# The recurrent mixer's three gate-branch subtractions, from VectorE to GpSimd

## The chip, the core and the metric

The kernel runs on one core of a Trainium2 chip. What counts is the device time of one execution in microseconds (us), taken as the median of several runs; lower is better. The core has TensorE (PE in the profile), VectorE (DVE), ScalarE (ACT) and GpSimd (POOL), and SyncE (SP), whose queue issues the transfers from memory.

## What is computed

Two blocks of two layers each work on 256 tokens of width 1024 in float32. The part that the change touches is the recurrent mixer of the first block, cut here to its core:

```python
def mixer_rglru(h, w_in, conv_w, conv_b, w_a, b_a, w_x, b_x, lam, w_out):
    gate, xr = jnp.split(h @ w_in, [D_RNN], axis=-1)
    gate = jax.nn.gelu(gate)
    xr = causal_conv(xr, conv_w) + conv_b
    r = sigmoid(einsum('bthi,hij->bthj', xh, w_a) + b_a)     # xh: xr by heads
    i = sigmoid(einsum('bthi,hij->bthj', xh, w_x) + b_x)
    log_a = (LRU_C * r) * log_sigmoid(lam)
    a = exp(log_a)
    b = sqrt(-expm1(2.0 * log_a)) * (i * xr)
    hseq = scan(a, b)                                        # h_t = a_t h_(t-1) + b_t
    return (gate * hseq) @ w_out
```

Before it stand another mixer and a mixture of 32 experts, behind it a second mixture of experts (`moe1`), and then the second block (feed-forward, attention and pooling).

## The kernel before

Five programs run side by side, one for each engine and one for the transfer queue, each a list of instructions in a fixed order. They meet at counting semaphores: an instruction raises one when it ends, and another engine's program waits for a count. Nothing plans the order at run time. What stands behind a waiting instruction on its own engine waits too.

**Chunks.** A dense weight comes in chunks of 128 x 2048 float32 (1 MB), into a ring of six places (`dense_ring`). Chunk n goes to place n modulo 6 once its predecessor there has been used. The mixer's chunks are named `("lru", n)`: 0 to 3 are the input columns of the convolution branch, then come `c_w_a` and `c_w_x`, 4 to 7 are the input columns of the gate branch, 8 to 11 the output matrix.

**High and low halves.** To multiply in near float32 accuracy, each chunk is split. ScalarE rounds it to `w_hi` (the helper `hi`, L923), then VectorE computes the chunk less its `w_hi` as `w_lo` (the helper `lo`, L1283): a `tensor_tensor` subtraction with both inputs and the output in SBUF. Each goes in two halves f = 0, 1 of 128 x 1024. There are two buffers for such pairs, used in turn, so `hi` of a chunk waits until TensorE has multiplied the same half of the chunk two turns earlier. TensorE makes three products for each piece (L445 to L447), and `tile_products` waits for `("remainder", key, f)` before each half; its 24 products for one half need both `w_hi` and `w_lo`.

**The mixer's order.** TensorE: chunks 0 to 3, chunk 4, the 32 gate products with `c_w_a` and `c_w_x` (L598), chunks 5, 6, 7, then the output chunks 8 to 11. VectorE (`lru` in `dve_program`): the norm; `lo` of 1; constants (`decay`); four times `lo` of chunk 2 + j and then the convolution of two channels, each one `tensor_scalar` (L1439) and three `scalar_tensor_tensor` (L1442) that read two SBUF tensors; then `lo` of 6; `factors` (L1449, L1451, L1452) for pairs 0 and 1; `lo` of 7; `factors` for pairs 2 and 3; `lo` of 8; the scans (L1460, L1462); the gating (L1467, L1289); `lo` of 9. ScalarE follows a like order: `hi` of chunk 2 + j and a copy of the products; `hi` of 6; a gelu (L1043); 16 tanh (L1065) once the last convolution channel, `("xr", 7)`, is there; `factors` 0 and 1 (tanh L1049, exponential L1054); `hi` of 7; `factors` 2 and 3; `hi` of 8; the square roots (L1074).

**GpSimd** has only sums of squares and, far later, the pooling. Ahead of the mixer its queue holds `first_sums("moe0")`, behind it `first_sums("moe1")`, two additions of 128 x 512 (L1878, L1880).

**The transfer queue** (`sp_program`) waits for `remainder` of a place's old chunk before it loads the next one: the load of 10 waits for 4, that of 11 for 5. The first three expert matrices of `moe1` in the dense ring (`EXTRA`) wait for 6 and 7, for 8 and 9, for 10 and 11. The rest of the experts' matrices start when TensorE has finished chunk 11 (L1982).

Of the kernel before, what the change touches and what calls it, by code (L numbers as in the profile page):

```python
# [161 lines left out]
def build(nc, a, out, known):  # L162
# [5 lines left out]
    def signal(name, step=1):  # L168
        s = Signal(nc, name, known, step)
        signals.append(s)  # L170
        return s
# [2 lines left out]
    rounded = signal("rounded")  # L174
    acted = signal("acted")
    remainder = signal("remainder")
    vec = signal("vec")
    pooled = signal("pooled")
    x_loaded, consts_loaded, small_loaded = (signal(n, 16) for n in ("x_loaded", "consts_loaded", "small_loaded"))
# [139 lines left out]
    halved = [key for key, _, split in chunks if split]  # L319
    turn = {key: n for n, key in enumerate(halved)}  # L320
    splits = set(halved)

    def slot(key):
        return dense_ring[place_of[key]]
# [110 lines left out]
    def pe_program(_):  # L435
# [38 lines left out]
        def tile_products(key, b, ready, x=h_halves, ks=range(KD)):  # L474
            w = weights(key)
            for f in range(2):
                PE.wait_ge(remainder, key, f)
                for n, k in enumerate(ks):
                    PE.wait_ge(*ready(k))
                    ins = triple(bank[b][:, f * T:(f + 1) * T], [v[:, f, k, :] for v in w],  # L480
                                 [v[:, k, :] for v in x], n == 0, n == KD - 1)
                ins.then_inc(products.up(key, f), 1)
# [796 lines left out]
    def dve_program(_):  # L1279
        def lo(key, halves=(0, 1)):  # L1280
            for f in halves:
                DVE.wait_ge(rounded, key, f)
                V.tensor_tensor(half_of(key, f, 1), tile_of(slot(key), key, f), half_of(key, f, 0).bitcast(F32),  # L1283
                                ALU.subtract).then_inc(remainder.up(key, f), 1)
# [145 lines left out]
        def lru():  # L1430
            norm("lru")
            lo(("lru", 1))
            seq(V.memset(lru_pad[:, :, 0:PAD_C], 0.0), "pad")
            decay()
            for j in range(4):
                lo(("lru", 2 + j))
                DVE.wait_ge(acted, "xr", j)
                for c in (2 * j, 2 * j + 1):
                    seq(V.tensor_scalar(lru_xr[:, c, :], lru_pad[:, c, 0:T], small_of("c_conv_w", c, 1),  # L1439
                                        small_of("c_conv_b", c, 1), ALU.mult, ALU.add))  # L1440
                    for tap in (1, 2, 3):
                        seq(V.scalar_tensor_tensor(lru_xr[:, c, :], lru_pad[:, c, tap:tap + T],  # L1442
                                                   small_of("c_conv_w", tap * KD + c, 1), lru_xr[:, c, :], ALU.mult, ALU.add),
                            *(("xr", c) if tap == 3 else ()))
            lo(("lru", 6))

            def factors(g):
                DVE.wait_ge(acted, "tanh", g, 1)
                seq(V.scalar_tensor_tensor(pair(lru_bx, g), pair(lru_bx, g), 1.0, pair(lru_xr, g), ALU.add, ALU.mult))  # L1449
                DVE.wait_ge(acted, "ra", g)  # L1450
                seq(V.tensor_tensor(pair(lru_xr, g), pair(lru_ra, g), pair(lru_ra, g), ALU.mult))  # L1451
                seq(V.scalar_tensor_tensor(pair(hT, g), pair(lru_xr, g), 1.0, pair(hT, g), ALU.add, ALU.mult), "factor", g)  # L1452

            for j in (1, 2):
                factors(2 * j - 2)
                factors(2 * j - 1)
                lo(("lru", 6 + j))
            for g in range(4):
                DVE.wait_ge(acted, "root", g)
                seq(V.tensor_tensor(pair(lru_bx, g), pair(lru_bx, g), pair(hT, g), ALU.mult), "bx", g)  # L1460
                for h in (2 * g, 2 * g + 1):
                    ins = V.tensor_tensor_scan(lru_xr[:, h, :], lru_ra[:, h, :], lru_bx[:, h, :], 0.0, ALU.mult, ALU.add)  # L1462
                    ins.then_inc(vec.up("scan", h), 1)
            DVE.wait_ge(vec, "scan", KD - 1)
            for g in range(4):
                DVE.wait_ge(acted, "gelu", g)
                V.tensor_tensor(pair(lru_gate, g), pair(lru_gate, g), pair(lru_xr, g), ALU.mult).then_inc(vec.up("gy", g), 1)  # L1467
                lo_pair(("gy", g), h_halves, lru_gate, g)
            lo(("lru", 9))
            project("lru", 8, [("lru", 10), ("lru", 11)], 0.5)  # L1470
# [372 lines left out]
    def pool_program(_):  # L1843
        def sums(s):

            q = [hflat[:, i * 2 * T:(i + 1) * 2 * T] for i in range(4)]
            POOL.wait_ge(acted, "sq", s, 1)
            if s != "f10":
                POOL.wait_ge(products, "ms", before[s])
            pool_seq(G.tensor_tensor(square_sum, q[0], q[1], ALU.add))  # L1850
            for i in (2, 3):
                POOL.wait_ge(acted, "sq", s, i)
                pool_seq(G.tensor_tensor(square_sum, square_sum, q[i], ALU.add), *(("ss", s) if i == 3 else ()))  # L1853

        def pools(s):

            if s == "m1":
                POOL.wait_ge(vec, "merged", "m0", 3)
            for buf in (uT, s2, s4):
                ins = G.memset(buf[:, :, 0:EDGE], 0.0)  # L1860
            pool_seq(ins, "edges", s)
            POOL.wait_ge(vec, "u", s, 4)
            src, dst = uT, s2
            for n, w in enumerate(WINDOWS):
                sh = w // 2
                pool_seq(G.tensor_tensor(dst[:, n:, EDGE:L], src[:, n:, EDGE:L], src[:, n:, EDGE - sh:L - sh], ALU.add))
                G.tensor_scalar(poolT[:, n, EDGE:], dst[:, n, 2 * EDGE:L], 1.0 / w, None, ALU.mult)
                pool_seq(G.tensor_tensor(poolT[:, n, 0:EDGE], dst[:, n, EDGE:2 * EDGE],
                                         C("rcount")[:, n * EDGE:(n + 1) * EDGE], ALU.mult))
                pool_seq(G.tensor_tensor(poolT[:, n, :], poolT[:, n, :], uT[:, n, EDGE:L], ALU.subtract),  # L1870
                         *(("pool", s) if n == 3 else ()))
                src, dst = dst, (s4 if dst is s2 else s2)

        def first_sums(s):

            q = [work[:, i * 2 * T:(i + 1) * 2 * T] for i in range(3)]
            POOL.wait_ge(acted, "sq", s, 1)
            pool_seq(G.tensor_tensor(square_sum, q[0], q[1], ALU.add))  # L1878
            POOL.wait_ge(acted, "sq", s, 2)
            pool_seq(G.tensor_tensor(square_sum, square_sum, q[2], ALU.add), "ss", s)  # L1880

        for s in ROUTED:
            first_sums(s)
        for s in LATER:
            sums(s)
            if s[0] == "m":
                pools(s)


    def sp_program(_):  # L1890
# [5 lines left out]
        def dense_load(n):  # L1896
            key = order[n]
            if n >= RING:
                old = order[n - RING]
                if old in splits:  # L1900
                    SP.wait_ge(remainder, old, 1)
                elif old[0] == "lru":
                    SP.wait_ge(products, "gate", 3, 1)
                elif old[1] == "pool_w":
                    SP.wait_ge(products, "poolY", old[0])
                else:
                    SP.wait_ge(products, "branch", old[0], 0 if old[1] == "wp" else 1, 2 * old[2] + 1)
            s = dense_loaded[n % RING]
            s.n += 16
            sync.dma_start(dense_ring[n % RING], a["dense"][n]).then_inc(s.sem, 16)  # L1910
            s.at[key] = s.n
# [61 lines left out]
        for l in range(2):  # L1973
            last = order.index(("ab", 13) if l == 0 else ("lru", 11)) + 1
            for n in range(done, last):
                dense_load(n)
            done = last
            for i, both in enumerate(EXTRA[l]):
                for d in both:
                    SP.wait_ge(remainder, [k for k in order[:last] if place_of[k] == d][-1], 1)  # L1980
                experts(l, 3 + i, 4 + i)
            SP.wait_ge(products, ("ab", 13) if l == 0 else ("lru", 11), 1)  # L1982
            experts(l, 6, N_MATRIX)
            next_chunks(l, done, done + 2)
            SP.wait_ge(vec, "flag", l)
            again(l, sync.value_load(most_tokens[0:1, l:l + 1], min_val=0, max_val=T))
            next_chunks(l, done + 2, done + RING)
            done += RING
            if l == 0:
                for i in range(3):  # L1990
                    SP.wait_ge(products, *last_of(0, "a", i))
                experts(1, 0, 3)
# [67 lines left out]
```

## Time and profile before

| | |
|---|---|
| median of 3 runs | 2272.7 us (2264.48 to 2273.84) |
| profiled execution | 2276.3 us, its span 2274.5 us |
| TensorE busy | 1938.4 us (85%) |
| VectorE busy | 952.2 us (42%) |
| ScalarE busy | 655.1 us (29%) |
| GpSimd busy | 69.5 us (3%), 64 instructions |
| data moved | 622.93 MB, mean 274 GB/s |

All times below are microseconds from the span's start. The mixer lies at about 597 to 706. A row of the timeline merges neighbouring instructions of one line (x2, x3); a row's duration is an instruction's own record, and the distance from one start to the next is what the engine's queue really took for it. "idle before <- releaser" names what ended an idle time.

### The profile page before, as it was taken

Reading aid. Unit: us, or ns where it says so; the run is one execution under the profiler, and the core shown is the slowest. Engines: PE = TensorE matmul, PEld = TensorE weight load, DVE = VectorE, ACT = ScalarE, POOL = GpSimd, SP = SyncE. Lnnn points to the kernel's source line nnn. Section 1 sums busy time; section 2 is a strip of 40 time slices with the busy share of each in tenths; the row PEclk is TensorE's granted clock in tenths of the full one; section 3 lists DMA queues with packets and bytes.
Section 4 is the critical chain, followed back from the end, with each engine's and each line's share of the span. In section 5 each row is a group of like instructions: output and inputs, shape, how many; then the busy total and the mean of one; then the engine's idle time right before and its main releaser. Section 6 shows DMA issues by size and latency. Waiting matters only on the chain.

```text
span 2274.5 us, 35530 instructions
## 1 busy us (share of the span) xinstructions
PE 1938.4 (85%) x16022; PEld 1605.8 (71%) x16022; DVE 952.2 (42%) x1317; ACT 655.1 (29%) x912; POOL 69.5 (3%) x64
## 2 busy tenths in 40 slices
PE   7887677667778876776769999999999999999999
PEld 7863333334578433333339999889999999989999
DVE  4721111111483111111136556656556556656555
ACT  4410000000362000000024445434445445434443
POOL 0000000000000000000000001200000000300000
PEclk9999998998888999899889999999999999999999
DMA  9379999999836999999975554344554554435551
GB/s 382 116 307 427 428 427 427 427 428 427 340 132 234 428 427 427 427 427 427 427 325 171 184 183 167 130 167 167 185 185 168 185 181 156 171 120 189 186 186 56
DMA packets 62975, 622.93 MB, mean 274 GB/s; under 512 B 10593, under 2 KB 11105, under 8 KB 12129
## 3 DMA queue, kind: packets, MB, share of 16 engines
q1 hardware_dynamic: 62816, 620.57, 69.1%
q8 instruction: 130, 2.13, 0.4%
q14 instruction: 29, 0.23, 0.0%
HBM read 619.50 MB, written 1.05 MB: 273 GB/s over the span
## 4 chain that ended last, share of the span: by engine, by line
PE 56%; DMA 22%; issue 10%; DVE 9%; ACT 2%; POOL 1%; SPq 0%; DVEq 0%; POOLq 0%; ACTq 0%
PE ps L445 13%; PE ps L446 12%; PE ps L447 12%; DMA expert_ring_a<-in_moe_w_down 8%; PE ps L657 6%; DMA expert_ring_b<-in_moe_w_down 6%; DMA dense_ring<-in_moe_w_down 6%; PE ps L645 5%; PE ps L634 3%; DMA expert_ring_a<-in_moe_w_up 2%; PE ps L668 2%; DVE w_lo L1283 2%; POOL work L1853 1%; DVE work L1442 1%; PE ps L454 0%
## 5 line engine op out<-in xcount | busy, mean ns | idle before, releaser
L1283 DVE TENSOR_TENSOR w_lo<-dense_ring,w_hi 128x1024 fp32r<-128x1024 f32 x384 | 477.5, 1259 | 374.1 <-ACT w_hi L923 373.6
L445 PE MATMUL ps<-h_hi,w_hi 128*128 128x256 f32 x2112 | 607.5, 288 | 27.8 <-DVE h_lo L1289 10.9
L446 PE MATMUL ps<-h_lo,w_hi 128*128 128x256 f32 x2112 | 602.4, 285 | 0.0
L447 PE MATMUL ps<-h_hi,w_lo 128*128 128x256 f32 x2112 | 602.1, 285 | 0.0
L923 ACT CAST w_hi<-dense_ring 128x1024 fp32r<-128x1024 f32 x384 | 395.7, 1045 | 317.5 <-PE ps L447 303.5
L445 PEld LDWEIGHTS ps<-h_hi,w_hi 128*128 128x128 f32 x2112 | 410.1, 194 | 33.2 <-issue 15.4
L446 PEld LDWEIGHTS ps<-h_lo,w_hi 128*128 128x128 f32 x2112 | 410.4, 194 | 0.3
L447 PEld LDWEIGHTS ps<-h_hi,w_lo 128*128 128x128 f32 x2112 | 410.2, 194 | 0.0
L1552 DVE TENSOR_TENSOR work<-work,ps 128x256 f32<-128x256 f32 x32 | 13.5, 421 | 541.6 <-ACT work L1109 541.6
L445 PE MATMUL ps<-hid_hi,w_hi 128*128 128x256 f32 x704 | 199.7, 284 | 0.0
L446 PE MATMUL ps<-hid_lo,w_hi 128*128 128x256 f32 x704 | 199.2, 283 | 0.0
L447 PE MATMUL ps<-hid_hi,w_lo 128*128 128x256 f32 x704 | 199.2, 283 | 0.0
L645 PE MATMUL ps<-dense_ring,work 128*32 128x256 f32 x1408 | 135.7, 420 | 42.0 <-DMA expert_ring_b<-in_moe_w_up 24.5
L645 PE MATMUL ps<-expert_ring_a,work 128*32 128x256 f32 x1408 | 138.7, 425 | 38.3 <-DMA dense_ring<-in_moe_w_up 24.5
L1109 ACT ACTIVATE work<-ps 128x256 f32<-128x256 f32 x32 | 12.3, 384 | 550.0 <-PE ps L645 550.0
L645 PE MATMUL ps<-expert_ring_b,work 128*32 128x256 f32 x1280 | 127.8, 414 | 36.9 <-DMA expert_ring_a<-in_moe_w_up 25.1
L657 PE MATMUL ps<-expert_ring_a,work 128*32 128x512 f32 x384 | 117.7, 688 | 23.0 <-DMA expert_ring_a<-in_moe_w_down 21.9
L445 PEld LDWEIGHTS ps<-hid_hi,w_hi 128*128 128x128 f32 x704 | 135.1, 192 | 0.4
L446 PEld LDWEIGHTS ps<-hid_lo,w_hi 128*128 128x128 f32 x704 | 135.1, 192 | 0.0
L447 PEld LDWEIGHTS ps<-hid_hi,w_lo 128*128 128x128 f32 x704 | 135.1, 192 | 0.0
L645 PEld LDWEIGHTS ps<-dense_ring,work 128*32 128x32 f32 x1408 | 76.5, 121 | 75.4 <-issue 54.2
L645 PEld LDWEIGHTS ps<-expert_ring_a,work 128*32 128x32 f32 x1408 | 76.2, 122 | 73.4 <-issue 52.4
(277 smaller groups left out, 2080.3 us busy)
## 6 DMA issues: line engine op xcount, KB each, us to landing
dense_ring<-in_dense SPq DMA_DIRECT2D x204, 1024.0 KB, 4.8
expert_ring_a<-in_moe_w_gate SPq DMA_DIRECT2D x24, 2048.0 KB, 30.7
dense_ring<-in_moe_w_up SPq DMA_DIRECT2D x24, 2048.0 KB, 31.0
expert_ring_a<-in_moe_w_down SPq DMA_DIRECT2D x24, 2048.0 KB, 32.9
expert_ring_a<-in_moe_w_up SPq DMA_DIRECT2D x20, 2048.0 KB, 34.6
dense_ring<-in_moe_w_down SPq DMA_DIRECT2D x20, 2048.0 KB, 32.4
expert_ring_b<-in_moe_w_gate SPq DMA_DIRECT2D x20, 2048.0 KB, 31.3
expert_ring_b<-in_moe_w_up SPq DMA_DIRECT2D x20, 2048.0 KB, 34.8
```

The lines of the kernel that those rows point to most:

```text
L445: mm(o, w[0], x[0], start=start, stop=False, **kw)
L446: mm(o, w[0], x[1], start=False, stop=False, **kw)
L447: return mm(o, w[1], x[0], start=False, stop=stop, **kw)
L634: ins = mm(bank[b][:, (k % 4) * P:(k % 4 + 1) * P], h_tok[:, tt * D + k * P:tt * D + (k + 1) * P], pick[:, tt * P:(tt + 1) * P], start=tt ...
L645: ins = mm(bank[2 + pr][c:c + CAP, m * half:(m + 1) * half], xs[:, k, (2 * pr + x) * CAP:(2 * pr + x + 1) * CAP], w[:, k, hf * half:(hf + ...
L657: ins = mm(bank[6 + n][r0:r0 + CAP, :], hidT[pr][:, c:c + CAP], w[:, f, n * 512:(n + 1) * 512], start=f == 0, stop=f == FE - 1)
L668: ins = mm(bank[b][:, j * T:(j + 1) * T], y_slots[:, (2 * q + j) * P:(2 * q + j + 1) * P], spread, start=True, stop=True)
L923: S.copy(half_of(key, f, 0), tile_of(slot(key), key, f)).then_inc(rounded.up(key, f), 1)
L1283: V.tensor_tensor(half_of(key, f, 1), tile_of(slot(key), key, f), half_of(key, f, 0).bitcast(F32), ALU.subtract).then_inc(remainder.up(key ...
L1442: seq(V.scalar_tensor_tensor(lru_xr[:, c, :], lru_pad[:, c, tap:tap + T], small_of("c_conv_w", tap * KD + c, 1), lru_xr[:, c, :], ALU.mult ...
L1552: return V.tensor_tensor(hid[pr], silu_g[pr], bank[2 + pr][:, D_EXP // 2:], ALU.mult)
L1853: pool_seq(G.tensor_tensor(square_sum, square_sum, q[i], ALU.add), *(("ss", s) if i == 3 else ()))
```

## The change

In `pool_program` a helper `lo` is added. GpSimd computes with it the low halves of chunks 5, 6 and 7, as six subtractions of 128 x 1024, between `first_sums("moe0")` and `first_sums("moe1")`. They raise a semaphore of their own, `remainder_g`. VectorE's three `lo` calls for these chunks go. TensorE's and the transfer queue's waits for these three chunks ask `remainder_g`, by `low_of`. Everything else stays.

```diff
+    remainder_g = signal("remainder_g")
+    BY_POOL = [("lru", 5), ("lru", 6), ("lru", 7)]
+
+    def low_of(key):
+        return remainder_g if key in BY_POOL else remainder
...
         def tile_products(key, b, ready, x=h_halves, ks=range(KD)):
             w = weights(key)
             for f in range(2):
-                PE.wait_ge(remainder, key, f)
+                PE.wait_ge(low_of(key), key, f)
...
             for j in range(4):
-                lo(("lru", 2 + j))
+                if j < 3:
+                    lo(("lru", 2 + j))
                 DVE.wait_ge(acted, "xr", j)
...
-            lo(("lru", 6))
-
             def factors(g):
...
                 factors(2 * j - 1)
-                lo(("lru", 6 + j))
+                if j == 2:
+                    lo(("lru", 8))
...
-        for s in ROUTED:
-            first_sums(s)
+        def lo(key):
+            for f in range(2):
+                POOL.wait_ge(rounded, key, f)
+                G.tensor_tensor(half_of(key, f, 1), tile_of(slot(key), key, f), half_of(key, f, 0).bitcast(F32),
+                                ALU.subtract).then_inc(remainder_g.up(key, f), 1)
+
+        first_sums("moe0")
+        for key in BY_POOL:
+            lo(key)
+        first_sums("moe1")
...
                 if old in splits:
-                    SP.wait_ge(remainder, old, 1)
+                    SP.wait_ge(low_of(old), old, 1)
...
                 for d in both:
-                    SP.wait_ge(remainder, [k for k in order[:last] if place_of[k] == d][-1], 1)
+                    old = [k for k in order[:last] if place_of[k] == d][-1]
+                    SP.wait_ge(low_of(old), old, 1)
```

## Rows read from the trace of the kernel before

**Rows 1.** Windows: us, then busy us of PE, PEld, DVE, ACT, POOL, clock, DMA, GB/s.
```profile
620.00:645.00 25.00, 21.48 (x160) 20.33 (x160) 23.86 (x41) 10.38 (x14) 0.00 (x0) 1.00 0.25 85
740.00:1165.00 425.00, 302.57 (x2766) 161.33 (x2764) 48.05 (x100) 16.57 (x36) 0.00 (x0) 0.90 1.01 427
```

**Rows 2.** Chain of work that ended last, in time order: start, us, what.
```profile
638.09 2.36 DVE w_lo L1283 x2
644.43 5.95 ACT work L1065 x16
...
657.49 2.36 DVE w_lo L1283 x2
664.12 2.36 DVE w_lo L1283 x2
```

**Rows 3.** Timeline of DVE, 630 to 654: start, us, engine, line, what, [idle before].
```profile
630.24 1.53 DVE L1442 SCALAR_TENSOR_TENSOR work<-work,small 128x256 f32<-128x256 f32 x3
634.08 0.41 DVE L1439 TENSOR_SCALAR work<-work,small 128x256 f32<-128x256 f32 x1
...
644.38 2.36 DVE L1283 TENSOR_TENSOR w_lo<-dense_ring,w_hi 128x1024 fp32r<-128x1024 f32 x2
...
653.87 0.69 DVE L1451 TENSOR_TENSOR work<-work 128x512 f32<-128x512 f32 x1 [6.53 <-ACT work L1054]
```

**Rows 4.** Timeline of ACT, 630 to 658.
```profile
630.07 1.05 ACT L923 CAST w_hi<-dense_ring 128x1024 fp32r<-128x1024 f32 x1 [1.99 <-PE ps L447]
632.89 1.04 ACT L923 CAST w_hi<-dense_ring 128x1024 fp32r<-128x1024 f32 x1 [1.77 <-PE ps L447]
637.71 1.05 ACT L923 CAST w_hi<-dense_ring 128x1024 fp32r<-128x1024 f32 x1 [3.29 <-PE ps L447]
640.53 1.05 ACT L923 CAST w_hi<-dense_ring 128x1024 fp32r<-128x1024 f32 x1 [1.77 <-PE ps L447]
644.43 5.95 ACT L1065 ACTIVATE work<-ps,work 128x256 f32<-128x256 f32 x16 [0.94 <-DVE work L1442]
655.78 1.98 ACT L923 CAST w_hi<-dense_ring 128x1024 fp32r<-128x1024 f32 x2
```

**Rows 5.** Timeline of PE around chunk 4, chunk 5 and the output chunks.
```profile
634.47 0.39 PE L445 MATMUL ps<-h_hi,w_hi 128*128 128x256 f32 x1 [1.62 <-ACT work L1038]
648.69 0.47 PE L445 MATMUL ps<-h_hi,w_hi 128*128 128x256 f32 x1
676.31 0.55 PE L445 MATMUL ps<-h_hi,w_hi 128*128 128x256 f32 x1 [10.00 <-DVE h_lo L1289]
```

**Rows 6.** Timelines of POOL and DVE where both work, 1181 to 1184.
```profile
1181.18 1.43 POOL L1850 TENSOR_TENSOR work<-hT 128x512 f32<-128x512 f32 x1 [478.96 <-ACT hT L966]
1181.38 1.52 DVE L1312 SCALAR_TENSOR_TENSOR h_lo<-xT,gain_both,h_hi 128x256 fp32r<-128x256 f32 x1
L1312 DVE SCALAR_TENSOR_TENSOR h_lo<-xT,gain_both,h_hi x8: 479/480/1522, 1179.0 to 1182.8; 128x256 fp32r<-128x256 f32 x8
```

**Rows 7.** The same two timelines, 1384 to 1388.
```profile
1384.75 2.13 POOL L1853 TENSOR_TENSOR work<-work,hT 128x512 f32<-128x512 f32 x1
1385.68 2.28 DVE L1283 TENSOR_TENSOR w_lo<-dense_ring,w_hi 128x1024 fp32r<-128x1024 f32 x1
```

**Rows 8.** The same two timelines, 1418 to 1422.
```profile
1418.27 1.89 POOL L1866 TENSOR_TENSOR scratch<-scratch 128x1024 f32<-128x1024 f32 x1 [31.01 <-DVE scratch L1801]
1418.35 3.17 DVE L1731 TENSOR_TENSOR scratch<-scratch,work 128x1280 f32<-128x1280 f32 x1
```

**Rows 9.** Lines by form: count, busy us, mean ns of one.
```profile
L1774 DVE TENSOR_TENSOR work<-work 128x2048 f32<-128x2048 f32 x2 | 4.6, 2292 | 0.1
...
L1774 DVE TENSOR_TENSOR work<-work 128x1024 f32<-128x1024 f32 x2 | 2.4, 1224 | 0.1
```

**Rows 10.** Timeline of POOL, the addition in the first `first_sums`.
```profile
113.94 1.30 POOL L1878 TENSOR_TENSOR work<-work 128x512 f32<-128x512 f32 x1 [113.51 <-ACT work L937]
```

**Rows 11.** Timeline of the transfer queue, 700 to 712.
```profile
706.07 0.81 SPq L1919 DMA_DIRECT2D expert_ring_b<-in_moe_w_gate  x2
```

## The prediction

> **What bounds the kernel now.** I read the windows first, then the chain of waits, then the engines' timelines. Most of the kernel lies outside the change. In `moe1`, from 740 to 1165, the transfers run at 427 GB/s with a DMA share of 1.01 [rows 1], so that stage takes the time of its data. Its stream of expert matrices starts when TensorE has finished the mixer's last output chunk, at 706.07 [rows 11]. So whatever moves the end of the mixer moves the rest of the kernel by as much, and the mixer's end is what has to be forecast.
>
> In the mixer the bound is VectorE: from 620 to 645 it is busy 23.86 of 25.00 us, GpSimd 0.00 [rows 1]. The chain of waits goes through its subtractions of chunk 5 (638.09), 7 (657.49) and 8 (664.12), each pair 2.36 us as recorded [rows 2]. The pair of chunk 6 (644.38) is not on it [rows 2, 3]: there the chain has passed to ScalarE's tanh at 644.43, which waited 0.94 us for the last convolution channel [rows 4]. VectorE then idles 6.53 us for ScalarE's exponential and goes on at 653.87 [rows 3]. So two engines take turns: VectorE until 644.4, ScalarE until 653.9, VectorE from there.
>
> **What the change removes.** Six subtractions leave VectorE. The convolution of pair 2 begins 2.28 us after the pair of 631.80 (634.08 against 631.80, where the three convolution steps of 630.24 end with their 1.53 us [rows 3]), so one half costs 1.14 us in the queue and a chunk 2.28 us. If that were all: channel 7 would be ready 2.28 us sooner, but ScalarE waited only 0.94 us for it, so ScalarE gains 0.94 us. The first `factors` end at 656.55 instead of 657.49. The pair of chunk 7 goes. The two `factors` behind it are six operations of (657.49 - 653.87) / 5 = 0.72 us each; the second waits for an exponential that ScalarE has ready about 1.3 us behind 657.6, which takes back most of what was freed. They end near 662.5 instead of 664.12, a gain of 1.6 us. That is the best that this change has in it, not 6.8 us.
>
> **What it adds: the subtraction on GpSimd, and what VectorE loses by it.** The trace of before has no GpSimd operation of this exact form (128 x 1024, in strips of 128, fp32r out). It has near ones, and it shows what they do to VectorE. While GpSimd's 512-wide addition of 1181.18 ran, a VectorE operation that takes 480 ns took 1522 ns [rows 6]: 1.04 us lost. The very subtraction of the change, on VectorE, took 2.28 us for one half during GpSimd's 512-wide addition [rows 7], where two halves otherwise take 2.36 us [rows 3], one thus 1.22: 1.06 us lost. And GpSimd's addition of 1384.75 took 2.13 us instead of the 1.30 of an undisturbed one [rows 7, 10], since VectorE was in the middle of an operation. During GpSimd's 1024-wide addition of 1418.27 VectorE's 1280-wide product took 3.17 us [rows 8]; by the slope of the 1024 and 2048 wide ones (1.224 and 2.292 us [rows 9], 1.04 ns an element) it should take 1.49, so 1.68 us were lost. So the two engines exclude each other when both read two tensors from SBUF: the one that comes second waits until the first has ended, and when both have more to do they alternate.
>
> The Trainium skill says the same ("SBUF — State Buffer", Who interferes with whom): a VectorE instruction with two SBUF inputs contends with a GpSimd instruction that reads SBUF, for the whole instruction, by order of issue. Rows 6 to 8 agree, with 1.04 to 1.68 us lost for one operation. It speaks against this change; a sum that leaves it out gives the 1.6 us of gain above.
>
> I call the time for which a 1024-wide GpSimd subtraction shuts VectorE out its hold. From below 1.68 us [rows 8], from above 2.60, twice the full 1.30 of a 512-wide addition [rows 10]. I take 2.1, twice the 1.04 to 1.06 lost to a 512-wide one [rows 6, 7], as those too have two separate inputs. [...] Beside it: the Trainium skill's "GPSIMD Engine Reference", section Performance versus the Vector engine, gives 4497 ns for a 2048-wide float32 addition; half of that, an estimate of 2.25 us, would make the sum below about a microsecond larger.
>
> **Where the six holds fall.** GpSimd starts a half when ScalarE has rounded it. All VectorE operations here but the `tensor_scalar` of 634.08's kind (one SBUF input) read two tensors.
>
> - Chunk 5, half 0: rounded at 630.07 + 1.05 = 631.12 [rows 4]. VectorE is in its last two steps of channel 3 [rows 3]; one step is pushed back by a hold. VectorE +2.1.
> - Chunk 5, half 1: rounded at 633.93 [rows 4]. VectorE is in half 0 of chunk 4 (now 633.9 to 635.0), GpSimd comes next, half 1 of chunk 4 begins at 637.15 and ends near 638.3 instead of 634.08 + 0.1. VectorE +4.2. TensorE starts chunk 4 at about 635.1 instead of 634.47 [rows 5], and its second half 0.9 us late; so the two roundings of chunk 6 come at 638.3 and 641.5 instead of 637.71 and 640.53 [rows 4].
> - Chunk 6, half 0: rounded at 639.4. VectorE is in channel 4, +2.1, now 6.3 behind.
> - Chunk 6, half 1: rounded at 642.5. VectorE has a `tensor_scalar` then, which overlaps; the step behind it waits 1.8. Now 8.1 behind.
>
> Channel 7 follows without the pair of chunk 5: 8.1 - 2.3 = 5.8 us later than before, at 650.2. ScalarE, ready since about 644.5, starts its tanh 5.8 us late, and TensorE's gate products, chunk 5 (648.69 before [rows 5]) and the rounding of chunk 7 (655.78 [rows 4]) move by the same 5.8. The freed time of chunk 6's pair lies before an idle stretch and is worth nothing.
>
> - Chunk 7: rounded at 662.6 and 663.6. VectorE begins the last two `factors` at 663.3. Half 0 takes 663.3 to 665.4, one VectorE operation follows, half 1 takes 666.1 to 668.2, and five operations of 0.72 end at 671.8. Before it was 664.12: 2.3 saved, two holds of 2.1 lost, 1.9 more behind. Sum 5.8 + 1.9 = 7.7 us.
>
> Chunk 8's subtraction, the scans, the gating and the output chunks hang on VectorE in a chain and move by 7.7. TensorE's wait of 10.00 us before the first output chunk [rows 5] only becomes some 2 us longer. TensorE needs chunk 7's halves at about 666 and 669, GpSimd delivers them at 665.4 and 668.2: no wait of its own, but with little to spare.
>
> **Edits that cost nothing.** Behind GpSimd's new waits stands only `first_sums("moe1")`, due after 689: 20 us of cover. The transfer queue waits for chunk 5 on GpSimd (done 637.2, before near 640.4), and for 6 and 7 (668.2 instead of 659.8); behind that wait stand expert matrices that `moe1` needs after 720. The semaphore itself is one count among many. If that cover were gone, the cost would be that of a late 2 MB transfer.
>
> **The sum.** Profiled execution 2276.3 + 7.7 = 2284.0; that execution stands 3.6 above the median of the runs, so 2272.7 + 7.7 = 2280.4 us, or 0.34% slower. By the hold of 1.68: six times 0.42 less, 5.2 us, 2277.9. By 2.60: six times 0.5 more, 10.7 us, 2283.4.
>
> **Rivals.**
> 1. No loss by exclusion, or GpSimd always gives way: then the gain is the 1.6 us worked out above, 2271.1. For it: VectorE works in short steps with gaps, 0.04 us between. Against it: rows 6 to 8, where each overlap cost VectorE the addition's length.
> 2. Slower by over 0.5%: this piece holds the port longer than the rows suggest, by its strips of 128 or its output type. Each further microsecond of hold costs about 6 us, so it decides from a hold of 2.7: 7.7 + 6 x 0.6 = 11.3. At a hold of 3.2 it is 14.3 us, 2287. Chunk 7 would then also come late for TensorE. For it: GpSimd's rate is uneven (1024 wide in 1.89 [rows 8], 512 wide in 1.30 [rows 10]). Against it: all these rows are under 2.1 of undisturbed length.
> 3. The whole VectorE relief arrives (6.8 us, 2265.9): that needs ScalarE not to be next. Rows 3 and 4 speak against it, with 0.94 us of wait on the one side and 6.53 on the other.
>
> **How the numbers follow.** Forecast 0.68 (hold between 1.68 and 2.60, 2277.9 to 2283.4). Rival 1: 0.09. Rival 2: 0.21. Rival 3: 0.02. The range of 8 in 10 takes in rival 2 up to a hold of 3.2 and goes below the forecast's lower end to the lower part of rival 1 and the spread of the runs: 2269 to 2288. A change of 0.5% (11.4 us) is about what can be told from none here; slower by more than that is rival 2 with the top of the forecast's interval, 0.23; faster by more needs rival 3 and luck, 0.03; within it 0.74.
>
> **What the new profile would show.** The six subtractions as rows of POOL between about 631 and 668, 1.7 to 2.6 us each where undisturbed. VectorE's convolution steps of 485 ns, four of them, with 2 us more, or one of chunk 4's halves above 3 us. Channel 7 and ScalarE's tanh near 650 instead of 644.4. The last `factors` operation ending near 671.8, and the expert stream starting near 713.8 instead of 706.07. The prediction is wrong if VectorE's durations stay at 0.48 and 1.22 us beside a running GpSimd, or if the tanh starts before 644.4.

## The result and the profile after

The changed kernel takes 2281.59 us (median of 12 runs, 2279.82 to 2285.07), the kernel before, run beside it, 2272.02 us (12 runs, 2264.44 to 2276.06). By the medians that is 9.6 us slower, or 0.42%. The ratio, which is taken over all the runs, is 1.0051 with a 95% interval of 1.0041 to 1.0061, which stands for 11.6 us (9.3 to 13.9). The forecast was 7.7 us slower, between 2277.9 and 2283.4. The measured median lies in that range; the 7.7 itself lies under the interval of the ratio.

Most of it can be read from a few rows. The timeline of GpSimd after, with the six subtractions (columns: start us, us, what, idle before and its releaser):

```profile
629.97 2.38 POOL L1892 TENSOR_TENSOR w_lo<-dense_ring,w_hi 128x1024 fp32r<-128x1024 f32 x1 [511.51 <-ACT w_hi L930]
632.71 3.41 POOL L1892 TENSOR_TENSOR w_lo<-dense_ring,w_hi 128x1024 fp32r<-128x1024 f32 x1 [0.37 <-ACT w_hi L930]
639.82 2.49 POOL L1892 TENSOR_TENSOR w_lo<-dense_ring,w_hi 128x1024 fp32r<-128x1024 f32 x1 [3.70 <-ACT w_hi L930]
642.67 2.35 POOL L1892 TENSOR_TENSOR w_lo<-dense_ring,w_hi 128x1024 fp32r<-128x1024 f32 x1 [0.35 <-ACT w_hi L930]
664.02 5.66 POOL L1892 TENSOR_TENSOR w_lo<-dense_ring,w_hi 128x1024 fp32r<-128x1024 f32 x2 [19.00 <-ACT w_hi L930]
```

The timeline of VectorE after, over the same time:

```profile
626.91 1.53 DVE L1450 SCALAR_TENSOR_TENSOR work<-work,small 128x256 f32<-128x256 f32 x3
...
628.92 3.70 DVE L1450 SCALAR_TENSOR_TENSOR work<-work,small 128x256 f32<-128x256 f32 x3
632.66 4.55 DVE L1290 TENSOR_TENSOR w_lo<-dense_ring,w_hi 128x1024 fp32r<-128x1024 f32 x2
...
639.58 5.72 DVE L1450 SCALAR_TENSOR_TENSOR work<-work,small 128x256 f32<-128x256 f32 x3
...
664.62 2.78 DVE L1455 SCALAR_TENSOR_TENSOR work<-work 128x512 f32<-128x512 f32 x1
667.43 2.79 DVE L1457 TENSOR_TENSOR work<-work 128x512 f32<-128x512 f32 x1
...
672.43 0.69 DVE L1458 SCALAR_TENSOR_TENSOR hT<-work,hT 128x512 f32<-128x512 f32 x1
673.16 2.36 DVE L1290 TENSOR_TENSOR w_lo<-dense_ring,w_hi 128x1024 fp32r<-128x1024 f32 x2
```

Read them together. The last row of GpSimd merges the two halves of chunk 7, about 2.83 us each. Three convolution steps take 1.53 us where GpSimd is idle, 3.70 us with one GpSimd subtraction beside them and 5.72 with two. The pair of chunk 4 takes 4.55 instead of 2.36 [rows 3], and two `factors` operations 2.78 and 2.79 us instead of 0.69. That is 2.17, 2.19, 4.19 (for two), 2.09 and 2.10 us lost: six holds of 2.1 to 2.2 us, 12.7 us in all, for 6.8 us of subtractions removed. The other side of it is GpSimd's second row: 3.41 us instead of 2.38, for it waited until VectorE's half of chunk 4 was done.

ScalarE's tanh and the queue behind the mixer, after (timelines of ScalarE and of the transfer queue), against [rows 4, 11]:

```profile
649.41 3.85 ACT L1072 ACTIVATE work<-ps,work 128x256 f32<-128x256 f32 x10 [4.91 <-DVE work L1450]
654.12 0.84 ACT L1072 ACTIVATE work<-ps,work 128x256 f32<-128x256 f32 x2 [0.87 <-PE ps L605]
655.80 1.70 ACT L1072 ACTIVATE work<-ps,work 128x256 f32<-128x256 f32 x4 [0.84 <-PE ps L605]
...
714.99 0.80 SPq L1934 DMA_DIRECT2D expert_ring_b<-in_moe_w_gate  x2
```

The 16 tanh are no longer one block of 5.95 us: twice ScalarE waits for TensorE, and from first to last they take 8.09 us. TensorE's own rows and the windows show why. The last 16 gate products, after and before (the bracket is the wait before them):

```profile
650.30 6.33 PE L605 MATMUL ps<-work,dense_ring 128*128 128x256 f32 x16 [5.33 <-ACT work L1072]
```

```profile
645.32 3.72 PE L598 MATMUL ps<-work,dense_ring 128*128 128x256 f32 x16 [1.37 <-ACT work L1065]
```

The windows (us, busy us of PE, PEld, DVE, ACT, POOL, granted clock, DMA share, GB/s); after:

```profile
645.00:650.00 5.00, 0.00 (x0) 0.00 (x0) 4.03 (x9) 0.59 (x2) 0.02 (x1) 0.88 0.00 0
650.00:656.50 6.50, 6.20 (x17) 5.02 (x18) 0.69 (x1) 4.79 (x13) 0.00 (x0) 0.57 0.00 0
```

and before:

```profile
644.00:645.30 1.30, 0.00 (x0) 0.00 (x0) 1.26 (x2) 0.87 (x3) 0.00 (x0) 1.00 0.00 0
645.30:649.00 3.70, 3.68 (x18) 3.27 (x19) 2.04 (x3) 3.70 (x11) 0.00 (x0) 1.00 0.00 0
```

TensorE waited 5.33 us for the first tanh instead of 1.37, and then ran its gate products at a mean granted clock of 0.57, near the lower of its two levels (1.2 GHz), where before it had 1.00 (2.4 GHz).

The same happened once before, at chunk 4, and did not reach ScalarE's tanh directly. TensorE waited 2.48 us for the low half there, where it had waited 1.62 us for ScalarE [rows 5], and about one microsecond into its products the clock fell. TensorE's first product of chunk 4 and a window behind it, after:

```profile
634.03 0.35 PE L452 MATMUL ps<-h_hi,w_hi 128*128 128x256 f32 x1 [2.48 <-DVE w_lo L1290]
...
635.00:638.50 3.50, 3.50 (x19) 3.50 (x19) 3.43 (x4) 0.00 (x0) 1.12 (x1) 0.52 0.02 5
```

and the window before:

```profile
635.40:638.90 3.50, 3.50 (x32) 3.50 (x31) 3.29 (x7) 1.05 (x1) 0.00 (x0) 1.00 0.03 7
```

To set traces side by side I measure from the mixer's norm, whose reciprocal starts at 601.66 before and 600.37 after. What lies ahead of it is the same work, and over all traces of this study this start differs by up to 2.6 us. The marks are the start of the first tanh, the time from the first to the end of the last, the start of the last `factors` operation, that of the last subtraction of the gating (L1289, after L1296), and the start of the expert stream:

| us from the norm's reciprocal | first tanh | 16 tanh | last `factors` | last gating | expert stream |
|---|---|---|---|---|---|
| before | 42.77 | 5.95 | 61.73 | 79.75 | 104.41 |
| after | 49.04 | 8.09 | 72.06 | 90.08 | 114.62 |
| difference | +6.27 | +2.14 | +10.33 | +10.33 | +10.21 |

The mixer is 10.2 us longer in these two traces; the medians differ by 9.6, and the ratio stands for 11.6. From the expert stream to the end of the span it is 1568.4 us before and 1564.3 after; over all traces of this study that rest varies from 1558.6 to 1569.3 without order. So the marks are the better ruler for parts of 1 or 2 us, and the timed ratio for the sum. Each kernel has one trace, though, so a mark is a single reading.

### The profile page after: what moved, and what is told of

It is laid out like the page before. It is cut to its first block, busy times and chain, and to the rows that moved or that the text cites. A ratio compares the mean times of both kernels' runs of the same rounds, so it can differ in the third digit from the quotient of the medians.

```text
span 2279.3 us, 35525 instructions
## 1 busy us (share of the span) xinstructions
PE 1938.7 (85%) x16018; PEld 1605.3 (70%) x16022; DVE 958.4 (42%) x1311; ACT 655.2 (29%) x912; POOL 85.8 (4%) x70
## 4 chain that ended last, share of the span: by engine, by line
PE 57%; DMA 22%; issue 10%; DVE 9%; ACT 2%; POOL 1%; SPq 0%; DVEq 0%; POOLq 0%; ACTq 0%
PE ps L452 13%; PE ps L453 13%; PE ps L454 13%; DMA expert_ring_a<-in_moe_w_down 8%; PE ps L664 6%; DMA expert_ring_b<-in_moe_w_down 6%; DMA dense_ring<-in_moe_w_down 6%; PE ps L652 5%; PE ps L641 3%; DMA expert_ring_a<-in_moe_w_up 2%; PE ps L675 2%; DVE w_lo L1290 2%; POOL work L1860 1%; DVE work L1450 1%; DVE h_lo L1319 0%
```

## The experiments

Each is compared with the kernel before, run on the same chip, or, where its text says so, by the marks.

**1. The relief without the cost.** Nobody computes the three chunks' low halves.

```diff
-        return remainder_g if key in BY_POOL else remainder
+        return rounded if key in BY_POOL else remainder
...
-                PE.wait_ge(low_of(key), key, f)
+                PE.wait_ge(rounded if key in BY_POOL else remainder, key, f)
...
-        for key in BY_POOL:
-            lo(key)
```

> The low halves of chunks 5, 6 and 7 are computed by nobody: VectorE's six subtractions are gone, GpSimd has none, and TensorE multiplies what the low buffers happen to hold, after the high half alone (so the result leaves out these terms). This is the change's relief without its cost. My theory (ScalarE is next as soon as VectorE is relieved): ScalarE's tanh starts 0.9 us sooner than in the kernel before, the last factors operation ends 1.6 us sooner, the median is 1.6 us under before (ratio 0.9993). The rival (all freed time of VectorE arrives): 6.8 us under before, ratio 0.997.

Measured: 2266.96 us against 2271.04, ratio 0.9987 (0.9971 to 1.0002), which leaves anything from no gain to 6.6 us of it. The marks tell more. By them, tanh 41.69 (1.08 sooner), last `factors` 60.14 (1.59 sooner), expert stream 103.92 (0.49 sooner). The last `factors` is where it was expected to the tenth. So the change's whole VectorE relief of 6.8 us was worth 1.6 us at that point: ScalarE was next. The timeline of ScalarE in this run shows no wait in front of the tanh, which is what "ScalarE is next" means:

```profile
641.96 5.95 ACT L1072 ACTIVATE work<-ps,work 128x256 f32<-128x256 f32 x16
```

Behind the gating another 1.1 us of it went: the output chunks took 25.76 us to the expert stream instead of 24.66. The windows from the start of `w_lo` of chunk 9 on, here, with 34 TensorE products in six us and a granted clock of 0.62:

```profile
679.37:685.37 6.00, 6.00 (x34) 6.00 (x35) 3.59 (x3) 2.19 (x3) 0.00 (x0) 0.62 0.46 137
```

and in the kernel before, 43 at 0.83:

```profile
682.35:688.35 6.00, 6.00 (x43) 6.00 (x44) 3.83 (x4) 3.28 (x4) 0.00 (x0) 0.83 0.42 128
```

TensorE comes out of its wait ahead of the output chunks (9.50 us here, 10.00 before) at the lower level in both; it comes back to the upper one sooner in one than in the other.

**2. GpSimd writes only.** As experiment 1, with three fills of zeros for each half on GpSimd. TensorE again waits only for the rounding.

```diff
-                G.tensor_tensor(half_of(key, f, 1), tile_of(slot(key), key, f), half_of(key, f, 0).bitcast(F32),
-                                ALU.subtract).then_inc(remainder_g.up(key, f), 1)
+                for n in range(2):
+                    pool_seq(G.memset(tile_of(slot(key), key, f), 0.0))
+                G.memset(tile_of(slot(key), key, f), 0.0).then_inc(remainder_g.up(key, f), 1)
```

> As the run without the three chunks' low halves, but GpSimd fills the place of each half in the ring three times with zeros (1024 wide, in strips of 128) at the points where it subtracted; it reads no tensor, and nothing waits for it but the loads. The result leaves out the low terms. My theory (the engines exclude each other only where GpSimd reads from SBUF beside a VectorE operation with two inputs): VectorE's convolution steps stay at 0.485 us and the time is that of the run with no work, 1.6 us under before. The rival (any GpSimd work on SBUF at these points shuts VectorE out): steps of 1.5 us and more, and some 3 to 8 us over before.

Measured: 2272.13 us against 2271.04, ratio 1.0001 (0.9985 to 1.0018). The interval holds both no change and the 1.6 us that were expected, so again the marks decide: tanh 41.92, last `factors` 60.39, within 0.3 us of the run with no work. GpSimd was busy for about as long as with its subtractions, so it is not GpSimd's being at work as such that costs the 2.1 us. The lines of the convolution in this run (duration in ns, smallest, median, largest):

```profile
L1450 DVE SCALAR_TENSOR_TENSOR work<-work,small x24: 483/485/486, 621.1 to 642.2; 128x256 f32<-128x256 f32 x24
...
L1447 DVE TENSOR_SCALAR work<-work,small x8: 406/432/1189, 620.6 to 640.7; 128x256 f32<-128x256 f32 x8
```

Not one of the 24 steps with two inputs was held up, as the theory had it. But the `tensor_scalar`, with one tensor input, was, twice: 1.19 and 1.02 us instead of 0.41. Two more that met a fill took 0.45. The prediction had called that kind free of it.

**3. GpSimd reads one tensor.** As experiment 2, with a product by 1.0 in place of the fills.

```diff
-                G.tensor_tensor(half_of(key, f, 1), tile_of(slot(key), key, f), half_of(key, f, 0).bitcast(F32),
-                                ALU.subtract).then_inc(remainder_g.up(key, f), 1)
+                G.tensor_scalar(tile_of(slot(key), key, f), tile_of(slot(key), key, f), 1.0, None,
+                                ALU.mult).then_inc(remainder_g.up(key, f), 1)
```

> As the run with the zeros, but GpSimd multiplies each half in its place in the ring by 1.0, one input instead of two, 1024 wide. The result leaves out the low terms. My theory (the exclusion is by GpSimd's reading): VectorE loses one hold for each of the six, as in the changed kernel, but by the length of a one-input operation. If that is 1.0 to 1.5 us, then six holds are 6 to 9 us less the relief, and the time is 2 to 6 us over before. The rival (only a GpSimd operation with two inputs excludes VectorE): 1.6 us under before.

Measured: 2274.00 us against 2271.04, ratio 1.0013 (0.9998 to 1.0028). By the medians that is 3.0 us over before, but the interval reaches down to no change; it leaves out the rival's 1.6 us under before. By the marks: tanh 43.44, last `factors` 62.61, expert stream 105.41, that is 1.0 us over before. The direction is the theory's; by the marks the size is less than expected. VectorE's timeline:

```profile
628.24 2.38 DVE L1450 SCALAR_TENSOR_TENSOR work<-work,small 128x256 f32<-128x256 f32 x3
...
632.94 1.13 DVE L1447 TENSOR_SCALAR work<-work,small 128x256 f32<-128x256 f32 x1
636.11 2.18 DVE L1450 SCALAR_TENSOR_TENSOR work<-work,small 128x256 f32<-128x256 f32 x3
```

GpSimd's own, in part of it:

```profile
629.31 2.77 POOL L1892 TENSOR_SCALAR dense_ring<-dense_ring 128x1024 f32<-128x1024 f32 x1 [510.84 <-ACT w_hi L930]
...
636.85 2.90 POOL L1892 TENSOR_SCALAR dense_ring<-dense_ring 128x1024 f32<-128x1024 f32 x1 [1.19 <-ACT w_hi L930]
```

VectorE lost 0.85, 0.72 and 0.65 us in these rows, and 0.72 three times more behind them: six holds for six operations. GpSimd records these operations as 2.77 and 2.90 us in the rows shown, and 2.76 to 3.61 over all six. So a GpSimd record is not the hold, and a single input held VectorE for about a third of what two inputs did. (It also wrote to the ring, as float32, where the subtraction writes to `w_lo`; no run parts these from the number of inputs.)

**4. TensorE's wait filled.** The changed kernel, with products of zeros in the wait.

```diff
+                    if g == 2 and m == 0:
+                        PE.wait_ge(vec, "zeros")
+                        PE.wait_ge(*emptied[7])
+                        for n in range(24):
+                            mm(bank[7], zeros[:, 0:P], zeros[:, :], start=True, stop=True)
                     claim(b, acted, "tanh", g, m)
```

> The changed kernel, whole, with 24 products of zeros (128x512 in bfloat16, into a bank not in use) put in front of the third pair's gate products on TensorE, to fill its wait of 5.33 us for ScalarE's first tanh. In the changed kernel the granted clock over the gate products of 650 to 656.5 was 0.57, against 1.00 in the kernel before, and ScalarE's 16 tanh took 8.0 us from first to last instead of 5.95. My theory (this is the part of the loss that the prediction lacked): with the wait filled the clock stays at 1.0, the tanh take 6.0 us again, and the time falls by 2 us against the changed kernel, to 7.5 us over before. The rival (the loss is not the clock's): as the changed kernel, 9.6 us over before, the tanh still at 8 us.

Measured: 2279.72 us against 2271.04, ratio 1.0042 (1.0023 to 1.0062). That interval overlaps the changed kernel's, so the time alone doesn't decide. The trace does: first tanh 49.02, as after, but the 16 take 5.94 us, and the last `factors` starts at 69.89, 2.17 us sooner than after. Window and timeline of ScalarE:

```profile
650.00:656.50 6.50, 6.35 (x40) 5.83 (x40) 0.69 (x1) 6.48 (x18) 0.00 (x0) 1.00 0.24 60
```

```profile
649.37 5.94 ACT L1077 ACTIVATE work<-ps,work 128x256 f32<-128x256 f32 x16 [4.91 <-DVE work L1455]
```

The clock stays at 1.00, and ScalarE no longer waits for TensorE between its tanh. The 2.1 us were the clock's. About 1.0 us of it was lost again behind the gating (25.51 us to the expert stream, after 24.54), where the clock came back later, as in experiment 1.

**5 to 7. One chunk at a time.** `BY_POOL` holds one key, and VectorE's two other `lo` calls stand as before.

```diff
-    BY_POOL = [("lru", 5), ("lru", 6), ("lru", 7)]
+    BY_POOL = [("lru", 6)]
```

> The kernel before with chunk 5 alone on GpSimd. Theory (each half that GpSimd subtracts shuts VectorE out for 2.1 us wherever VectorE is busy): two holds of 2.1, one pair of 2.28 saved, so ScalarE's tanh and all behind it 1.9 us later than before; TensorE waits 1.9 us longer before the gate products, and if the clock falls in that, up to 2 us more. 1.9 to 3.9 us over before. Rival (moving a subtraction away is worth its 2.28 us, only chunk 6 and 7 cost): 0.9 us under before.

> The kernel before with chunk 6 alone on GpSimd. VectorE's own pair stood ahead of an idle stretch of 6.5 us, so nothing that decides is saved; the two holds fall into chunk 5's pair and the last convolution channels. Theory with the clock: tanh 4.2 us later, and the gate products behind a wait of over 5 us at a low clock, 2 us more: 6.2 us over before. Rival (the holds alone, without the clock): 4.2 us over before. Rival (chunk 6 costs nothing as it had an idle stretch to go to): no change.

> The kernel before with chunk 7 alone on GpSimd. Theory: the tanh start as before; the last factors operation ends 1.9 us later (two holds of 2.1 less the pair of 2.28), and so does the mixer: 1.9 us over before. With the other two single moves this should add up to the 10.3 us by which the changed kernel's trace is longer from the norm to the last factors. Rival (chunk 7's halves come too late for TensorE, which is what costs): TensorE waits for them, more than 3 us over before.

Measured, with the differences to before in brackets:

| | ratio (95%) | first tanh | 16 tanh | last `factors` | expert stream |
|---|---|---|---|---|---|
| chunk 5 | 1.0027 (1.0013 to 1.0041) | 44.82 (+2.05) | 5.94 | 63.78 (+2.05) | 107.11 (+2.70) |
| chunk 6 | 1.0052 (1.0034 to 1.0071) | 46.97 (+4.20) | 8.19 | 68.18 (+6.45) | 111.61 (+7.20) |
| chunk 7 | 1.0006 (0.9990 to 1.0022) | 42.75 (-0.02) | 5.94 | 63.63 (+1.90) | 107.16 (+2.75) |

At the last `factors` the three add up: 2.05 + 6.45 + 1.90 = 10.40, where all together gave 10.33. At the expert stream they do not (12.65 against 10.21), as each of the three took 0.7 to 0.9 us longer over the output chunks than before. The timed ratios add up no better: they stand for 6.1, 11.8 and 1.4 us, where all together gave 11.6. Chunk 6 alone is nearly two thirds of it, and it is the chunk whose subtraction cost VectorE no time that counted, as it stood ahead of an idle 6.5 us. VectorE and GpSimd in that run:

```profile
638.21 4.55 DVE L1290 TENSOR_TENSOR w_lo<-dense_ring,w_hi 128x1024 fp32r<-128x1024 f32 x2
...
642.68 2.43 DVE L1446 TENSOR_SCALAR work<-work,small 128x256 f32<-128x256 f32 x1
```

```profile
639.02 5.95 POOL L1890 TENSOR_TENSOR w_lo<-dense_ring,w_hi 128x1024 fp32r<-128x1024 f32 x2 [520.77 <-ACT w_hi L930]
```

One hold falls into chunk 5's pair (4.55 us instead of 2.36), the other onto a `tensor_scalar` with one tensor input, 2.43 us instead of 0.41: it is shut out like the rest. The tanh are 4.20 us late, two holds, and take 8.19 us, with the granted clock at 0.57 from 650 to 656 again. With chunk 5 alone TensorE waited 1.15 us for the first tanh, before 1.37, and the 16 took 5.94: no long wait there, and no loss by the clock in the tanh. (Behind its 2.47 us of wait at chunk 4 the clock fell as in the changed kernel, to 0.55 from 635.0 to 638.4.) TensorE never waited for chunk 7's halves from GpSimd in that run or in the changed kernel, so the late delivery that the expectation for chunk 7 named as a rival is out. The timed ratio of chunk 6's run, with four executions, lies above its marks (interval 7.7 to 16 us, against 7.2), and that of chunk 7 below. The rest of the kernel varies by several us, so I go by the marks; that the parts add up is shown by them alone, and only as far as the last `factors`.

**8. VectorE's own order.** The kernel before, nothing on GpSimd.

```diff
             for j in range(4):
-                lo(("lru", 2 + j))
+                if j < 3:
+                    lo(("lru", 2 + j))
...
+            lo(("lru", 5))
             lo(("lru", 6))
...
-                lo(("lru", 6 + j))
+                if j == 1:
+                    lo(("lru", 7))
...
+                if g < 2:
+                    lo(("lru", 8), (g,))
```

> The kernel before with nothing on GpSimd, but VectorE's own order changed: chunk 5's pair behind the last convolution channel, where VectorE goes on to wait for ScalarE, and chunk 8's two halves each between a gating product and the subtraction behind it, where VectorE waits 0.68 us for ScalarE's rounding. Theory: the tanh start 0.9 us sooner, and chunk 8's 2.28 us give back 1.36 as two waits of 0.68 are filled: 2.3 us under before (ratio 0.9990), of which the clock of the output products may take back about 1 us, as in the run without the three chunks. Rival (freed time is lost again behind ScalarE): no change.

Measured: 2270.72 us against 2271.17, ratio 1.0003 (0.9989 to 1.0017): no difference that can be measured, though the interval still holds the expected 0.9990. By the marks the tanh start 1.04 us sooner, but the last gating is only 0.79 sooner and not 2.3. The row that shows where chunk 8's gain went is VectorE's first scan product:

```profile
663.61 0.69 DVE L1463 TENSOR_TENSOR work<-work,hT 128x512 f32<-128x512 f32 x1 [1.84 <-ACT hT L1074]
```

Chunk 8's pair had hidden a wait for ScalarE's square root, which now stands open. The expectation had put that pair down as a cost on the chain; most of it was cover. The expert stream is 1.75 us sooner than before, but 0.96 of that is the output chunks' 23.70 us, the clock again.

**9 and 10. The wait ahead of the output chunks filled,** in the kernel before and in the reordered one.

```diff
+            PE.wait_ge(vec, "zeros")
+            PE.wait_ge(*emptied[0])
+            for n in range(44):
+                mm(bank[0], zeros[:, 0:P], zeros[:, :], start=True, stop=True)
             project("lru", 8, lambda k: (remainder, "gy", k // 2))
```

> The kernel before with 44 products of zeros (128x512 in bfloat16, into a bank not in use) on TensorE between chunk 7 and the output chunks, to fill its wait of 10.00 us. In the kernel before the granted clock was 0.50 over the first products of the output chunks and 0.83 over the six us behind. Theory (from the last gating subtraction to the start of the expert stream the trace took 24.66 us before, 25.76 in the run without the three chunks, 23.70 in the reordered one, and these differ by when the clock comes back): with the wait filled it is 23.3 us, so 1.3 us under before. Rival (the products are not what this stretch waits for): 24.7 us as before.

> The reordered kernel (chunk 5's pair behind the convolution, chunk 8's halves in the waits of the gating; nothing on GpSimd) with the 44 products of zeros ahead of the output chunks. Theory: from the norm to the start of the expert stream 102.2 us, where before had 104.41, the reordered one 102.66 and the changed one 114.62; the median 2 us under before (ratio 0.999), at the edge of what five rounds can tell. Rival (either part undoes the other): 103.5 us or more from the norm to the stream.

Measured: 2269.70 us against 2270.62, ratio 0.9996 (0.9977 to 1.0016), and 2271.48 against 2270.62, ratio 1.0004 (0.9989 to 1.0019). With the fill alone the granted clock was 1.00 throughout and the output chunks took 23.68 us instead of 24.66; the expert stream started at 103.43, 0.98 sooner, where 1.3 had been expected. In the combined kernel it started at 104.64, later than before, and the output chunks took 25.66. There the clock was full when the first output product came and fell after it, in the short waits between the gating's pairs (windows of this run):

```profile
664.00:676.00 12.00, 11.08 (x55) 5.45 (x55) 11.50 (x17) 5.89 (x10) 0.00 (x0) 1.00 0.08 34
676.00:684.00 8.00, 5.81 (x27) 5.31 (x28) 6.12 (x9) 4.17 (x5) 0.00 (x0) 0.66 0.00 0
```

So the rival of the tenth held, by way of the clock. Neither version beats the kernel before by more than can be measured.

## Why the prediction was right, and where it was not

- **The end of the mixer moves the rest.** Held within what can be told: the mark moved 10.2 us, the median 9.6, the ratio 11.6 (9.3 to 13.9).
- **The relief is 1.6 us, not 6.8.** Held: experiment 1 gives 1.59 at the last `factors`.
- **The exclusion, and a hold of 2.1 us.** Held: 2.09 to 2.19, at all six (two of them read as a pair, 4.19). The strips of 128 and the rounded output of rival 2 added nothing to it. The choice between 1.68 and 2.60 by the nearest rows [rows 6, 7] was right; the uneven 1024-wide row [rows 8] would have misled. Alternation held too, with GpSimd's 3.41 us. One reading was too strong: that each overlap "cost VectorE the addition's length". It cost 1.04 us for a record of 1.43 [rows 6], and here 2.1 for records of 2.35 to 2.49, so the hold is somewhat shorter than GpSimd's record. Experiment 2 shows that for operations with two inputs it is GpSimd's reading that counts, which is what the Trainium skill says ("SBUF — State Buffer", Who interferes with whom).
- **The first tanh 5.8 us late.** It was 6.27. The fourth hold had been put at 1.8 us as a `tensor_scalar` would run beside it; it fell wholly on a step with two inputs. The premise itself, that a `tensor_scalar` with one SBUF input is free of GpSimd, is wrong: it took 2.43 us instead of 0.41 beside a subtraction (chunk 6 alone), 1.13 beside a one-input operation, 1.19 beside fills.
- **Chunk 6 rounded 0.6 and 1.0 us later than before.** It was 2.28 and 2.31 us later by the marks: the forecast moved the start of chunk 4's products and not their length, and these ran at 0.52 of the clock for 3.5 us. Both holds of chunk 6 then fell on the steps of 639.58. It is the same omission as the next one, in a place where it added nothing to the tanh's start: 6.27 us is the four holds (8.55 us) less the 2.28 saved.
- **The tanh and the gate products "move by the same 5.8".** This is the step that failed. They did not move, they stretched: TensorE's longer wait let its clock fall, the gate products fed ScalarE too slowly, and the 16 tanh took 2.1 us more. Experiments 4 and 6 show it, the first by taking it away, the second by raising it with two holds alone. The rows for it were at hand: the prediction read TensorE's wait of 10.00 us [rows 5] and did not ask what a longer wait does to what follows.
- **Chunk 7: 1.9 us.** Held: 1.90 alone.
- **The sum.** 5.8 + 1.9 = 7.7 forecast; 6.27 + 2.14 + 1.92 = 10.33 by the marks (1.92: two holds of 2.1 less 2.28); 9.6 by the medians. The mechanism of the holds was right, the first term was 0.5 us small, and one of 2.1 us, the clock's, was missing. That the result still lies in the range is partly luck: the range was 3 us wide above the forecast to allow for a longer hold, the hold was not longer, and the missing term used that room.
- **The rivals.** No loss by exclusion, and the full relief, are out. The slower rival named a longer hold as its cause, decisive from 2.7 us. The hold stayed at 2.1, so the rival is out as a mechanism, yet the ratio came out at its 0.5%, 1.0051, by the clock (the medians at 0.42%).

For chunk 7's halves the prediction had "no wait of its own, but with little to spare": TensorE showed none.

What stays open: why the clock comes back at different times after the same kind of wait, and why single-input operations on either side hold or are held for other lengths. Over the traces the output chunks took 23.7 to 25.8 us, and which it will be was not forecast right in experiments 8 and 10.

## What to carry to other kernels

Work moved from VectorE to GpSimd does not run beside VectorE's work where the two shut each other out, as here with both reading from SBUF: look in the trace for a place where the two overlap already and read how much longer VectorE's operation became, then multiply by the number of operations, and set that against what is freed. Before counting what is freed, ask who is next and whether the operation stood ahead of an idle stretch, where it is free; chunk 6 was such an operation, and moving it cost the most. And when a change makes TensorE wait longer, what follows the wait is to be costed at the lower clock too.

## What the runs showed of the hardware

- A 128x1024 float32 subtraction on GpSimd took 2.35 to 2.49 us in three of six records, 2.83 and 3.41 in those in turn with VectorE, and shut VectorE's two-input operations out for 2.1 to 2.2 us each; for GpSimd's 512-wide additions it was 1.04 to 1.06 [rows 6, 7].
- A one-input GpSimd operation of the same size recorded 2.76 to 3.61 us, yet VectorE lost only 0.65 to 0.85.
- GpSimd's fills did not hold up VectorE's operations with two inputs, but did its `tensor_scalar` with one, for 0.6 and 0.8 us in two of four; a two-input subtraction on GpSimd held the same `tensor_scalar` for 2.0 us.
- TensorE behind a wait of 5.33 us had a mean granted clock of 0.57 over the next 6.5 us; behind 1.37 us, and behind 2.06 us with the one-input operations, it kept 1.00 over the same products. At chunk 4 it kept 1.00 behind 1.62 us and fell to a mean of 0.52 over 3.5 us behind 2.48. Products of zeros in the wait kept it at 1.00. In the combined kernel it fell to a mean of 0.66 over 8 us although such products had filled the long wait; behind them TensorE had waited 1.30 and 1.00 us between the gating's pairs.
